# Eight chunks of a split input at 2048 + 32 bytes instead of 2048

## The reference

```python
def swiglu(h, wg, wu, wd):
    return (jax.nn.silu(h @ wg) * (h @ wu)) @ wd

# every sub-layer: x <- x + w * post_norm(f(pre_norm(x))), w = 1/2 for the FFNs
# layer 0: FFN -> [NSA || DSA attention] -> memory cross-attention -> FFN
# layer 1: FFN -> [MLA || differential attention] -> memory cross-attention -> FFN
def rmsnorm(x, g):
    y = x32 * lax.rsqrt(jnp.mean(x32 * x32, axis=-1, keepdims=True) + RMS_EPS)
    return (y * g.astype(jnp.float32)).astype(x.dtype)
```

## Time and profile before

| | |
|---|---|
| median of three runs | 2361.34 us |
| the profiled execution, its time | 2359.32 us |
| the same, span from first to last instruction | 2357.2 us |
| mean granted TensorE clock | 0.979 of full speed |
| TensorE matmuls | 11594 |
| HBM | 89 GB/s over the span |

### The profile page before, as it was taken

How to read it: one execution, slowest core, us unless ns; L and a number is a source line. 1 busy time by engine, 2 the same in 40 slices (tenths; PEclk the granted TensorE clock), 3 DMA queues, 4 the chain that set the end, 5 groups by cost and what they waited for, 6 DMA issues and landing times.

```text
span 2357.2 us, 32909 instructions
## 1 busy us (share of the span) xinstructions
PE 2245.7 (95%) x11594; PEld 1895.7 (80%) x11598; DVE 1231.7 (52%) x2377; ACT 542.4 (23%) x1313; POOL 1358.3 (58%) x843
## 2 busy tenths in 40 slices
PE   6999999898989899999999999999989989999997
PEld 5888888687878798888888888888767879888886
DVE  5544324678876556553246445124477655745323
ACT  2111003216751441010031000013256144111000
POOL 5666665471147457666667666666330745766662
PEclk9999999799999999999999999999989999999998
DMA  5433332220023113333323333333211321333331
GB/s 193 166 98 98 90 98 73 103 72 19 24 78 115 54 53 109 98 96 93 98 80 99 98 98 89 95 93 103 68 39 38 108 63 46 109 96 97 91 99 52
DMA packets 62145, 205.60 MB, mean 87 GB/s; under 512 B 6815, under 2 KB 9247, under 8 KB 61652
## 3 DMA queue, kind: packets, MB, share of 16 engines
q1 hardware_dynamic: 55312, 187.86, 26.5%
q10 hardware_dynamic: 6724, 16.29, 2.0%
HBM read 201.98 MB, written 8.70 MB: 89 GB/s over the span
## 4 chain that ended last, share of the span: by engine, by line
PE 86%; DVE 7%; ACT 2%; issue 2%; POOL 1%; DMA 0%; another core or an unknown queue 0%; SPq 0%; ACTq 0%; POOLq 0%; DVEq 0%
PE bank L735 26%; PE bank L737 25%; PE bank L736 25%; PE bank L1004 3%; PE bank L987 2%; PE bank L973 1%; DVE h_lo L1609 1%; POOL sq_sum L629 1%; DVE ev_logit L1796 1%; PE bank L1054 1%; PE bank L763 1%; DVE bank L1670 1%; PE bank L787 1%; DVE od_logit L1796 1%; PE bank L970 1%
## 5 line engine op out<-in xcount | busy, mean ns | idle before, releaser
L605 POOL TENSOR_TENSOR w_lo<-w_raw,w_hi 128x1024 fp32r<-128x1024 f32 (+1 forms) x358 | 866.1, 2419 | 29.9
L735 PE MATMUL bank<-h_hi,w_hi 128*128 128x512 f32 (+1 forms) x2136 | 803.6, 376 | 28.3 <-DVE h_lo L1609 11.6
L736 PE MATMUL bank<-h_lo,w_hi 128*128 128x512 f32 (+1 forms) x2136 | 796.9, 373 | 0.0
L737 PE MATMUL bank<-h_hi,w_lo 128*128 128x512 f32 (+1 forms) x2136 | 796.7, 373 | 0.0
L603 POOL TENSOR_SCALAR w_hi<-w_raw 128x1024 fp32r<-128x1024 f32 (+1 forms) x358 | 382.7, 1069 | 709.4 <-PE bank L737 563.0
L735 PEld LDWEIGHTS bank<-h_hi,w_hi 128*128 128x128 f32 x2136 | 407.9, 191 | 105.9 <-issue 14.8
L737 PEld LDWEIGHTS bank<-h_hi,w_lo 128*128 128x128 f32 x2136 | 407.5, 191 | 70.0
L736 PEld LDWEIGHTS bank<-h_lo,w_hi 128*128 128x128 f32 x2136 | 408.2, 191 | 67.9
L735 PE MATMUL bank<-act_hi,w_hi 128*128 128x512 f32 (+1 forms) x792 | 290.1, 366 | 0.0
L736 PE MATMUL bank<-act_lo,w_hi 128*128 128x512 f32 (+1 forms) x792 | 289.4, 365 | 0.0
L737 PE MATMUL bank<-act_hi,w_lo 128*128 128x512 f32 (+1 forms) x792 | 289.4, 365 | 0.0
(11 more groups left out here) (264 smaller groups left out, 2416.9 us busy)
## 6 DMA issues: line engine op xcount, KB each, us to landing
w_raw<-in_w_up SPq DMA_DIRECT2D x176, 512.0 KB, 3.6
w_raw<-in_w_down SPq DMA_DIRECT2D x64, 448.0 KB, 3.3
w_raw<-in_w_down SPq DMA_DIRECT2D x32, 512.0 KB, 3.5
w_raw<-in_w_ev_in SPq DMA_DIRECT2D x19, 512.0 KB, 3.6
w_raw<-in_w_xkv SPq DMA_DIRECT2D x16, 512.0 KB, 3.6
w_raw<-in_w_od_in SPq DMA_DIRECT2D x16, 512.0 KB, 3.6
bias_line_rows<-bias_lines ACTq DMA_DIRECT2D x1, 6400.0 KB
ev_strip<-bias_line_rows ACTq DMA_DIRECT2D x16, 256.0 KB, 3.0
```

Source lines behind the costliest of these rows:

```text
L605: pool.tensor_tensor(w_lo[j][:, 0:cols], raw[j][:, 0:cols], w_hi[j][:, 0:cols].bitcast(F32), ALU.subtract).then_inc(split_done, 1)
L735: pe.matmul(out, w_hi[j][:, w], hi, start=first, stop=False)
L736: pe.matmul(out, w_hi[j][:, w], lo, start=False, stop=False)
L737: return pe.matmul(out, w_lo[j][:, w], hi, start=False, stop=last)
```

## The change

The three tensors h_hi, h_lo and y_ffn are allocated with 520 instead of 512 elements per chunk, and everything uses the first 512 of each. Chunks are then 2080 bytes apart, and begin at eight different remainders by 256. The last eight elements of each chunk are never touched.

```diff
+STEP_COLS = 8
...
     at_h = keep.at
-    h_hi = keep.put("h_hi", [P, KC, T], F32R)
-    h_lo = keep.put("h_lo", [P, KC, T], F32R)
-    y_ffn = Region(at_h).put("y_ffn", [P, KC, T], F32)
+    h_hi = keep.put("h_hi", [P, KC, T + STEP_COLS], F32R)[:, :, 0:T]
+    h_lo = keep.put("h_lo", [P, KC, T + STEP_COLS], F32R)[:, :, 0:T]
+    y_ffn = Region(at_h).put("y_ffn", [P, KC, T + STEP_COLS], F32)[:, :, 0:T]
```

## The result

The changed kernel takes 2385.05 us (median of four, 2383.06 to 2393.77) against 2359.35 us before. The ratio is 1.0113, 95% interval 1.0089 to 1.0138: it is slower by about 25 us, outside the predicted range. The profiled execution took 2383.71 us with a span of 2381.6, 24.4 us more than before's.

What follows compares the result with a forecast made beforehand. The prediction took TensorE's matmul pace in `product`, 226.7 ns per 512 columns, to bound the kernel. Its two terms, 0 and 0, left the time at 2361 us, range 2353 to 2370, with chance 0.73 of no measurable change.

Steps and rivals of the forecast that it cites:

- What bounds the kernel, how many matmuls, the price of 1 ns: The pace of `product` sets the end; 5607 h matmuls begin elsewhere, and one nanosecond on each is 5.6 us.
- Term 1: TensorE's moving reads of h in `product`: 0 expected, +-1.4 ns per matmul, or +-7.9 us.
- row (a): Attention P.V matmuls, 128x128, operand shifted by 128 bytes in one layer: 112 against 111 ns, read as no cost.
- Row (b): Compression matmuls of 62 columns at sixteen remainders: 58.5 and 58.3 ns a step, no start stands out.
- That speaks against it: Verdict on moving read and weight load colliding: attention P.V pace is alike at offsets 128 and 0 from the weights.
- the faster rival: In h products, equal remainders make moving read and weight load clash, costing 13.3 ns; losing it gives 2286 us; chance 0.10.
- Seven in eight: Chunk 0 keeps its address, so about seven in eight h matmuls, 5607 of 6408, would be affected.
- The slower rival: Chunks 1 to 7: runs starting off a 256-byte boundary need an extra piece, 3.3 ns, 2380 us, or more; chance 0.13.
- The other engines' traffic doesn't matter: In two 100 us stretches TensorE starts 443 matmuls each, with VectorE busy 50.9 or 20.8 us.
- Term 2: VectorE and ScalarE accesses to h and y_ffn: 0 expected, at most -1.0 to +0.8 us over 260 operations.
- The extra 13.3 ns: Time per `product` matmul beyond its columns at 2.4 GHz, taken as the only part an address change could win.
- The rule about ports: TensorE and ScalarE have own memory ports, only VectorE and GpSimd arbitrate, so addresses would win nothing.

Runs made afterwards that it cites:

- e5: Small kernel without the decoder, 48 matmuls in a row for each choice of moving and weight starts; steps of 226.7 to 240.0 ns for 512 fp32r columns.
- e9: Small kernel without the decoder, 48 matmuls in a row with 32 to 128 weight columns and other widths; 229.9 to 237.8 ns with 32 weight columns.
- e2: Kernel before with all of h 32 bytes further, chunks still 2048 bytes apart, weights unmoved; ratio 1.0144, 2392.43 us.
- e3: Kernel before with everything in the on-chip memory 32 bytes further, weights and x too; ratio 0.9992.
- e6: Kernel before with h and the weights 32 bytes further, act at its old remainder; ratio 1.0049, 2371.16 us.
- e7: Changed kernel with h_lo's chunks back at 2048 bytes apart, so the change for h_hi and y_ffn alone; ratio 1.0107, 2384.64 us.
- e12: Kernel before with only chunk 3 of h_hi, h_lo and y_ffn at a remainder 32 bytes off; ratio 1.0027, 2367.39 us.
- e4: Small kernel without the decoder, 24 matmuls in a row per choice of starts; 226.5 ns with h chunks 2048 bytes apart, 233 with 2048 + 32.
- e14: Small kernel without the decoder, moving operand or weights at step 0, or bf16 at several steps; 218.7 ns with moving step 0, bf16 215.8.
- e10: Kernel before with the weights 228 bytes further, for a better place of the 256-column products; ratio 1.0064.

## Why the prediction was wrong

- *What bounds the kernel, how many matmuls, the price of 1 ns.* Right. The pace of `product` sets the end, and a few nanoseconds on it came out as 25 us: 5256 full products by 5.8 ns are 30.5 us. The span grew by 24.4. Half h products became a little quicker, from 119.7 to 118.2 ns on average over the trace, 1.7 us for 1152 of them. What covers the other 4 us isn't shown.
- *Term 1, the step that failed.* I took 0 +-1.4 ns per matmul from rows 6 and 7; 5.8 was measured on full products. Neither row could have shown the effect, for two reasons. Both are plain fp32, not fp32r: rows 7 has 64 matmuls where the kernel issues 32, the mark of plain fp32, and e5 has this type at 429.2 ns at every start even with 512 columns. And row (a) has 128 columns; e9 shows that fp32r ones of that width stay at 111.7 ns at every start, 0, 32 and 180 alike. Row (b), with 62 columns, I had called weak for its shortness, and called (a) nearer. The bound that I made of them was none. The trace of before held no full-width fp32r product with another difference, and I should have said that it bounds nothing. The last sentence of the prediction, that it would fail by a grain finer than 128 bytes, doesn't name the reason either: e5 has 233.3 ns at the very 128 that (a) shows.
- *"That speaks against it"*, of a meeting between the moving read and the weights' read: wrong by the same row. Their relation is what counts (e2, e3, e6). But the faster rival had the sign wrong: equal remainders are the best place for 512 columns, not the clash. Nor are the 13.3 ns a fixed price at the start of a read: the best half product has 6.7 (e5).
- *Seven in eight.* Wrong. Chunk 0 is as slow as the others, since the lag of one matmul is carried over the next ones (e7, e12).
- *The slower rival* had the right side and nearly the size (2380), with a wrong mechanism: a piece more for a start off a boundary of 256 bytes. e3 moves every start off by 32 and costs nothing. Its lower price, 8 columns or 3.3 ns, was a guess at a size.
- *The other engines' traffic doesn't matter*: right. e4 shows the same steps with the other engines idle.
- *Term 2.* Right. The waits for h_lo at the seams are the same after the change (waits of TensorE, after; before in rows 5):

```profile
PE bank L736 <- DVE h_lo L1610: 11.6, 4, 3.6
...
PE bank L736 <- DVE h_lo L1685: 8.3, 13, 1.1
...
PE bank L736 <- DVE h_lo L1833: 5.6, 4, 1.4
```

- *The extra 13.3 ns.* I read them as the only thing that could be won, and forgot that it could be lost more of. At the lower clock there were none of them, and e14's bf16 has 2.5 at 2 bytes per column, 12.5 at 4, and twice the time at 8. This agrees with the thought that it is the demand per time that matters.
- *The rule about ports.* From the Trainium skill, SBUF — State Buffer, section "SBUF: two separate sides", I took that addresses would win nothing, since TensorE has ports of its own. That section speaks of contention between engines. What I took from the same page's note on lines, that starts at multiples of 32 lose nothing, didn't hold either: e5 has 2.2 to 7.7 ns more there. The Trainium skill, TensorE: Matmul & The Clock Gate, section "Step-by-step: what each phase is for", gives TensorE two independent read ports, one for the moving operand and one for the weights. The runs differ for fp32r: in e6 the steps follow the weights' start against the moving one. The measurement decides; for bf16 e14 saw no dependence on the moving start.

What stays open: what the two reads share. A clash paid only by the length of the weight load is excluded (e9), and so is a boundary of more than 32 bytes at which a read must begin (e3). That a lag is carried from one matmul to the next and settles at 226.7 ns only at certain differences was seen (e4, e5, e12); why at those wasn't found. Nor do the runs tell whether a moving read meets its own weights or the load of the next ones.

## What to carry to other kernels

Where TensorE runs fp32r products of 512 columns back to back at 2.4 GHz, put moving operand and weights at the same remainder by 256, and let chunk and tile steps be multiples of 256. Padding or shifting one of them by 32 bytes cost 2.6 to 2.9% of these matmuls' time (232.5 and 233.3 ns), padding both by 32 still 1.6% (e5), shifting all together by 32 nothing (e3), by 16 some 1.5% (e4). Read the pace from starts 24 or more apart, since 6 ns per matmul can't be seen in a single duration. And an unchanged pace in short matmuls is no evidence for long ones: first ask whether the row has the type and the width that could have shown the effect at all.

## What the runs showed of the hardware

- The step of fp32r matmuls with 512 columns depends, for starts at multiples of 32 that stay the same, on moving start minus weights' start, by 256: 226.7 ns at 0, 228.9 to 234.4 at the other multiples of 32, up to 240.0 at other starts (e5); in the decoder 232.5 with mixed differences, 233.3 at 32 and at -32 (e2, e6).
- With 256 columns the best place is another one: 113.3 ns at 192 against 120.0 at 0 (e5).
- bf16: 215.8 ns at every start, 451.7 at 8 bytes per column; one repeated word in fp32r: 218.7 ns (e14). 128 columns of fp32r: 111.7 ns at every start (e9). Plain fp32: 429.2 ns for each of two matmuls, at every start (e5).
- GpSimd's subtraction w_lo takes 2.42 us, and 2.05 with w_hi and w_lo 228 bytes further (e10).
